# Sample search rounds moved behind a head's masks, summed in the next head; rank sums moved ahead in the last part

## The chip, the cores and the metric

One core of one Trainium2 chip runs the whole program. Its engines are TensorE (PE: matmuls, and weight loads, PEld), VectorE (DVE), ScalarE (ACT), GpSimd (POOL) and SyncE (SP, which issues DMAs). Each runs its own list of instructions in order, and they wait for one another by semaphores. The metric is the device time of one execution in microseconds (us).

## The reference

One step of a hybrid decoder layer on 2048 new tokens of a prompt and on 8 sample tokens that have 4096 cached keys each:

```python
def indexer_scores(q_idx, w_idx, k_idx, valid):
    dots = jnp.einsum("bqhd,bld->bqhl", q_idx, k_idx, preferred_element_type=jnp.float32) * (IDX_DIM ** -0.5)
    s = jnp.einsum("bqh,bqhl->bql", w_idx.astype(jnp.float32) * (N_IDX_HEADS ** -0.5), jax.nn.relu(dots))
    return jnp.where(valid, s, -jnp.inf)
...
    # prompt, by blocks of 128 queries; sample alike, its keys found through a page table
    _, sel = lax.top_k(scores, n_sel)            # n_sel = 256
    att = attend_selected(q, k_sel, v_sel, ...)  # softmax over the selected keys, 8 heads
    conv = z["b_conv"] * short_conv(u_ext, conv_w)
    mo = mem_attend(z["q_mem"], mk, mv)          # 256 memory tokens, 4 heads
    o = concat([att * silu(z["g_att"]), conv * silu(z["g_conv"]), mo * silu(z["g_mem"])]) @ w_out
    return x + rms_norm(o, g_post)
```

The selection of 256 keys is not done by sorting. A threshold is searched bit by bit: count the scores that are not below a candidate, then keep or drop the bit. For the sample, the 4097 scores of each of 8 tokens lie spread over the 128 partitions, so each round of its search has two halves: VectorE counts per partition, and TensorE adds the counts of a token's partitions with a matmul by a matrix of blocks.

## The kernel before

The program has three stretches. The first projects all tokens. The second, on which most of this change works, takes the prompt in 16 parts of 128 queries (j = 0 to 15). The third, called the last part here, finishes the sample. Nothing but the order of each engine's own list and the semaphores sets when things run: the order is written by hand in `b_vector` and `b_tensor` (second stretch) and in `c_vector` and `c_tensor` (last part), with tables that say how many search steps go where.

**A part's heads.** For each of the 8 attention heads h of a part TensorE computes scores of head h+2 (h+1 from part 8 on) into PSUM (L1637). VectorE adds the mask and takes the row maximum (`mask`, L1392, and L1397, which makes the bias of the exponential). ScalarE does the exponential (L1235). TensorE turns the result by transposes (L1647), ScalarE copies the turned blocks out of PSUM (L1216), and TensorE multiplies them with the values (L1655). The probabilities lie in two buffers, so the mask of head h+1 waits for the transposes of head h-1. In head 3 TensorE also turns the memory attention (L1789), into one of the two PSUM slots that the transposes use. VectorE frees it with `gate_mem` (L1482), the first thing that it does in `behind` of head 4.

**What VectorE has besides.** `behind` holds the masks of the next head and a portion of search steps for a later prompt block (L1429, L1432, L1435 a step; select steps at L265 to L290). `normalise` (L1369) scales the output row of the part before, in head 3; GpSimd then adds the residual (L1199), and SyncE stores the row. `take_keys` (L1514, L1518) reads the sample's key products in parts 0 to 2. `decode_round` is one half round of the sample's search, in parts 3 to 7: take the sum of the last round (L1873), set the bit (L1874, L1875), count again (two of L1853), tell TensorE. There are 32 counts, seven in a part and four in part 7. TensorE's half, `decode_total` (L1679), stands at the end of a head, behind its transposes.

**A part's tail.** After head 7 TensorE does the gate products of the next part (L1624), the next block's index products (L1610), the memory scores (L1706) and the output projection (L1715), which all in all keep it busy. VectorE accumulates index scores and does further search steps.

**The last part.** VectorE compares all scores of the sample with the found threshold (L1978, L1980), TensorE sums the counts over partitions (L2125, L2126), VectorE breaks ties by a scan (L1988 to L1998), TensorE sums again (L2129, L2131), VectorE ranks the chosen keys (L2002 to L2007). Then, once ScalarE has gated the sample's projections (L1912, L1913), it prepares the table of chosen places (L2010 to L2026) and builds 64 one-hot blocks (L2048), by which TensorE compacts the places. The gather of keys and values, the attention and the projection follow in a chain. In TensorE's list the gate products of the sample (L2113, 64 matmuls in float32, 128 instructions) and 32 transposes of the memory keys (L2122) stand ahead of the two rank sums.

Of the kernel before, what the change touches and what calls it, by code (L numbers as in the profile page):

```python
# [16 lines left out]
P = 128  # L17
SEQ, D, HD = 2048, 1024, 64
NT = SEQ // P
KD = D // P  # L20
# [1308 lines left out]
def b_vector(dve, m, s):  # L1329
# [208 lines left out]
    def tail(j):  # L1538
        todo = search_steps(j, 1)
        if j >= 0:  # L1540
            take_keys(key_units(j, NH - 1))
            take_att(j)
        for x in range(8):
            behind(j, portion(todo, 8, x) if j < NT - 2 else todo if x == 5 else [], True)
            accumulate(j, x)
            if j + 1 < NT:
                if x == 1:
                    gates(j + 1, 0)
                if x == 3:
                    gates(j + 1, 1)  # L1550
            if x == 3 and j >= 0:
                gate_att(j)
            if x == 3 and j + 1 < NT:
                memory(j + 1)
# [5 lines left out]
    for j in range(NT):  # L1560
# [3 lines left out]
        for h in range(NH):  # L1564
            if h >= 1:
                take_keys(key_units(j, h - 1))
            decode_round(j, h)
# [9 lines left out]
            if h == 3 and j >= 1:  # L1577
                normalise(j - 1)
        tail(j)
# [5 lines left out]
def b_tensor(pe, m, s):  # L1585
# [164 lines left out]
    for j in range(NT):  # L1750
# [19 lines left out]
        for h in range(NH):  # L1770
            if h + ahead < NH:
                scores_of(j, h + ahead)
            for n in key_units(j, h):
                turn_keys(n)
                if before:
                    before()
                before = lambda n=n: times_keys(n)
# [6 lines left out]
            decode_total(j, h)  # L1784
# [316 lines left out]
def c_tensor(pe, m, s):  # L2101
# [9 lines left out]
    for n in range(8 * KD):  # L2111
        b, k = n // KD, n % KD
        mm = pe.matmul(m.bank[3][:, 8 * b:8 * b + 8], m.w2[:, k, b * P:(b + 1) * P], m.xts[:, k, :],  # L2113
                       start=(k == 0), stop=(k == KD - 1))
    mm.then_inc(s.c_z, 1)
# [8 lines left out]
    pe.wait_ge(s.c_sel, 1)  # L2124
    pe.matmul(m.bank[5][:, 4:6], con("blk"), m.cn[:], start=True, stop=True)  # L2125
    pe.matmul(m.bank[5][:, 6:8], con("low"), m.ce[:], start=True, stop=True).then_inc(s.c_off, 1)  # L2126
    pe.wait_ge(s.c_rank_ready, 1)
    for g in range(2):
        pe.matmul(m.bank[5][0:64, 10:11], con("seln")[:, 64 * g:64 * g + 64], m.nsel[:, g:g + 1], start=(g == 0),  # L2129
                  stop=(g == 1))  # L2130
    pe.matmul(m.bank[5][:, 8:10], con("low"), m.cn[:], start=True, stop=True).then_inc(s.c_off2, 1)  # L2131
# [410 lines left out]
```

## Time and profile before

| | us |
|---|---|
| median of three timed runs | 2460.67 (2460.06 to 2463.07) |
| the profiled execution: its own time | 2456.39 |
| its span, from the first to the last instruction | 2454.6 |
| TensorE busy, of the span | 2164.9 |
| VectorE busy | 1414.3 |
| ScalarE busy | 1202.7 |
| granted TensorE clock, mean over the span | 0.878 |

Busy time is a sum over stretches with different limits. The granted clock is 1.0 at 2.4 GHz and 0.5 at 1.2 GHz; a mean between them is a mixture in time. A row of the timeline gives the start in us from the start of the span, the length, the engine and line, and in brackets how long the engine was idle before it and what ended that. A matmul in float32 shows as two instructions.

### The profile page before, as it was taken

What the parts mean: (1) busy time and instruction counts of PE and PEld (TensorE: products, weight loads), DVE (VectorE), ACT (ScalarE), POOL (GpSimd) and SP (SyncE); (2) the same over time, 40 slices, a digit from 0 to 9 for tenths busy, and PEclk for the clock granted to TensorE, in tenths of its full rate; (3) what the DMA queues carried; (4) which work ended last, traced back from release to release, by engine and by line L of the source; (5) the groups of instructions that cost most, each with busy time, mean ns of one, the idle gap of its engine ahead of it and who ended that gap; (6) DMA issues with size and microseconds to landing.
All of it is one profiled execution on the core that took longest, in us unless ns stands there. A gap on an engine that the chain in (4) does not pass through costs nothing. (4 is left out here: it accounts for less than half of the span.)

```text
span 2454.6 us, 33475 instructions
## 1 busy us (share of the span) xinstructions
PE 2164.9 (88%) x12592; PEld 1747.5 (71%) x12592; DVE 1414.3 (58%) x3186; ACT 1202.7 (49%) x2337; POOL 120.5 (5%) x182
## 2 busy tenths in 40 slices
PE   7999999989996889989899898799999889899765
PEld 4776776767765867768678677587687777878662
DVE  2334776667734575675776866557865654343180
ACT  1112467778721345635564565656666566644100
POOL 0000000000000110000000000000000000000004
PEclk9999999999996899986887899789989888898656
DMA  7113121121115423021111110111100100000201
GB/s 276 72 51 102 65 78 54 68 85 45 63 28 199 129 63 107 14 61 48 33 50 39 46 31 32 43 49 46 34 33 20 59 20 29 26 20 23 78 5 31
DMA packets 63344, 144.61 MB, mean 59 GB/s; under 512 B 14456, under 2 KB 28960, under 8 KB 63184
## 3 DMA queue, kind: packets, MB, share of 16 engines
q1 hardware_dynamic: 59856, 131.99, 16.1%
q0 software_dynamic: 3328, 10.49, 1.4%
q8 instruction: 100, 1.64, 0.3%
q14 instruction: 60, 0.49, 0.1%
HBM read 100.22 MB, written 42.24 MB: 58 GB/s over the span
## 5 line engine op out<-in xcount | busy, mean ns | idle before, releaser
L1655 PE MATMUL psum<-sb_v,sb_ptb 128*128 128x64 f32 x2176 | 349.8, 313 | 32.9 <-ACT sb_ptb L1216 32.4
L1655 PEld LDWEIGHTS psum<-sb_v,sb_ptb 128*128 128x128 f32 x2176 | 338.8, 235 | 44.9 <-ACT sb_ptb L1216 44.5
L1216 ACT ACTIVATE sb_ptb<-psum 128x512 f32<-128x512 f32 (+3 forms) x384 | 202.7, 542 | 308.1 <-PE psum L1647 304.2
L819 PE MATMUL psum<-sb_w,sb_xt 128*128 128x512 f32 (+5 forms) x1088 | 337.7, 466 | 0.5 <-DVE sb_xt L552 0.5
L1647 PE MATMUL psum<-sb_con,sb_p 128*128 128x128 f32 x1328 | 247.8, 315 | 52.7 <-ACT sb_p L1235 25.2
L819 PEld LDWEIGHTS psum<-sb_w,sb_xt 128*128 128x128 f32 (+1 forms) x1088 | 183.0, 189 | 127.5 <-issue 114.3
L1647 PEld LDWEIGHTS psum<-sb_con,sb_p 128*128 128x128 f32 x1328 | 184.3, 172 | 84.0 <-ACT sb_p L1235 40.6
L858 PE MATMUL psum<-sb_xt,sb_w 128*128 128x128 f32 x2048 | 237.3, 275 | 0.0
L1392 DVE CUSTOM_DVE_ANT_0 sb_p<-psum,sb_bias 128x1024 f32<-128x1024 f32 (+7 forms) x128 | 126.6, 989 | 190.8 <-PE psum L1637 179.7
L858 PEld LDWEIGHTS psum<-sb_xt,sb_w 128*128 128x128 f32 x2048 | 234.3, 192 | 1.1
L1715 PE MATMUL psum<-sb_wo,sb_mix 128*128 128x512 f32 x512 | 232.4, 597 | 0.0
L297 ACT ACTIVATE sb_lowj<-sb_sc,sb_l_ncand,sb_l_scl 128x1152 bf16<-128x1152 f32 (+7 forms) x128 | 219.7, 1716 | 1.9
L1637 PE MATMUL psum<-sb_ks,sb_qa 128*128 128x512 f32 (+3 forms) x640 | 188.9, 435 | 12.0 <-DVE sb_mx L1392 7.9
L1235 ACT ACTIVATE sb_p<-sb_p,sb_nmax 128x128 f32<-128x128 f32 (+15 forms) x128 | 153.4, 1199 | 68.8 <-DVE sb_nmax L1397 68.5
L1610 PE MATMUL psum<-sb_ks,sb_qi 128*128 128x512 f32 (+3 forms) x448 | 141.4, 434 | 31.1 <-DMA sb_qi<-qt_s 23.1
L1429 DVE TENSOR_SCALAR_CACHE_REDUCE sb_r<-sb_sc,sb_l_c 128x2048 bf16<-128x2048 f32 (+7 forms) x84 | 161.8, 1926 | 0.9
L1715 PEld LDWEIGHTS psum<-sb_wo,sb_mix 128*128 128x128 f32 x512 | 94.9, 191 | 93.7 <-issue 92.5
L1637 PEld LDWEIGHTS psum<-sb_ks,sb_qa 128*128 128x128 f32 x640 | 133.2, 226 | 37.4 <-issue 9.9
L1624 PE MATMUL psum<-sb_p,sb_w 128*128 128x128 f32 x1152 | 145.6, 285 | 0.4
L1624 PEld LDWEIGHTS psum<-sb_p,sb_w 128*128 128x128 f32 x1152 | 143.0, 200 | 4.1 <-issue 0.9
L1610 PEld LDWEIGHTS psum<-sb_ks,sb_qi 128*128 128x128 f32 x448 | 80.7, 195 | 76.1 <-issue 45.9
L1624 PE MATMUL psum<-sb_qa,sb_w 128*128 128x128 f32 x896 | 112.5, 288 | 0.7
(408 smaller groups left out, 2929.3 us busy)
## 6 DMA issues: line engine op xcount, KB each, us to landing
qt_s<-sb_qt SPq DMA_DIRECT2D x32, 512.0 KB, 2.9
sb_x<-in_x_prompt SPq DMA_DIRECT2D x16, 512.0 KB, 4.6
xt_s<-sb_xt SPq DMA_DIRECT2D x16, 512.0 KB, 2.6
sb_qa<-qt_s SPq DMA_DIRECT2D x16, 512.0 KB, 3.6
sb_qa<-qt_s SPq DMA_DIRECT2D x32, 256.0 KB, 4.9
sb_xres<-in_x_prompt SPq DMA_DIRECT2D x16, 512.0 KB, 4.2
out_y_prompt<-sb_y SPq DMA_DIRECT2D x16, 512.0 KB, 2.9
sb_p<-xt_s SPq DMA_DIRECT2D x9, 512.0 KB, 5.6
```

The source lines that it names most:

```text
L297: return act.activation(junk, sc, ACT.Sign, bias=f.ncand[:, p], scale=f.scl[:, p], accum_out=f.tally[:])
L819: mm = pe.matmul(out, m.xt[:, p, k, 0:n], m.w1[:, k, lo:hi], start=(k == 0), stop=(k == KD - 1))
L858: mm = pe.matmul(m.pc[bank][:, j * P:(j + 1) * P], m.w1[:, k, lo:lo + P], m.xt[:, p, k, :], start=(k == 0), stop=(k == KD - 1))
L1216: act.activation(m.ptb[:, g, 0:cols], m.turn[slot][:, 0:cols], ACT.Copy).then_inc(s.t_act, 1)
L1235: act.activation(m.p[:, h % 2, 0:w], m.p[:, h % 2, 0:w], ACT.Exp, bias=m.nmax[:, h:h + 1], scale=SCALE, accum_out=m.l[:, h:h + 1]).then_in ...
L1429: ch.inc(dve.tensor_scalar(junk, sc, f.c[:, p], 0.0, ALU.is_ge, ALU.add, accum_out=f.cnt[:]))
L1610: mm = pe.matmul(m.score2(at)[:, lo:lo + n], m.qi[:, x, h, :], m.ks[:, 0, c[0] + lo:c[0] + lo + n], start=(x == 0), stop=(x == 1))
L1624: mm = pe.matmul(m.turn[slot][:, (b % 4) * P:(b % 4 + 1) * P], m.w2[:, k, b * P:(b + 1) * P], m.xt2(j)[:, k, :], start=(k == 0), stop=(k = ...
L1637: mm = pe.matmul(m.score2(slot)[:, lo:lo + n], m.qa[:, x, h, :], m.ks[:, kv, c[0] + lo:c[0] + lo + n], start=(x == 0), stop=(x == 1))
L1647: mm = pe.transpose(m.turn[slot][:, x * P:(x + 1) * P], src[:, lo + x * P:lo + (x + 1) * P], ident)
L1655: mm = pe.matmul(o, m.ptb[:, g, x * P:(x + 1) * P], v, start=st, stop=sp)
L1715: mm = pe.matmul(m.ybank[:, 512 * x:512 * x + 512], m.mix[:, k, :], m.wo[:, k, 512 * x:512 * x + 512], start=(n == 0), stop=(n == KD - 1))
```

## The change

`decode_round(j, h)` and `take_keys` move from the front of head h to its end, behind the masks of head h+1, the search steps and `normalise`. `take_keys` now names the keys of its own head rather than of the head before; as it stands behind the masks instead of ahead of the next ones, its instructions keep their places. `normalise` moves from head 3 to head 6 in parts 1 to 5. In TensorE's list `decode_total(j, h - 1)` stands in head h behind the scores and ahead of the transposes, where `decode_total(j, h)` stood behind them. In the last part the first rank sum comes ahead of the gate products, the second after 24 of the 64.

```diff
--- before.py
+++ after.py
@@ -1538,7 +1538,6 @@
     def tail(j):
         todo = search_steps(j, 1)
         if j >= 0:
-            take_keys(key_units(j, NH - 1))
             take_att(j)
         for x in range(8):
             behind(j, portion(todo, 8, x) if j < NT - 2 else todo if x == 5 else [], True)
@@ -1562,9 +1561,6 @@
             mask(j, 0, x)
         todo = search_steps(j, 0)
         for h in range(NH):
-            if h >= 1:
-                take_keys(key_units(j, h - 1))
-            decode_round(j, h)
             behind(j, portion(todo, NH, h), False, h + 1 if h + 1 < NH else None)
             if h == 0:
 
@@ -1574,8 +1570,10 @@
                 dve.tensor_tensor(m.mo[:].rearrange("p (h d) -> p h d", h=NMH),
                                   m.mobank.rearrange("p (h d) -> p h d", h=NMH),
                                   m.ml[:].unsqueeze(2).to_broadcast([P, NMH, HD]), ALU.mult).then_inc(s.mo, 1)
-            if h == 3 and j >= 1:
+            if h == (6 if j < 6 else 3) and j >= 1:
                 normalise(j - 1)
+            take_keys(key_units(j, h))
+            decode_round(j, h)
         tail(j)
     decode = c_prepare(dve, m, s, cf)
     normalise(NT - 1)
@@ -1770,6 +1768,7 @@
         for h in range(NH):
             if h + ahead < NH:
                 scores_of(j, h + ahead)
+            decode_total(j, h - 1)
             for n in key_units(j, h):
                 turn_keys(n)
                 if before:
@@ -1781,7 +1780,6 @@
                 if before:
                     before()
                 before = lambda h=h, c=c: times_values(j, h, c)
-            decode_total(j, h)
             if h == 3:
                 pe.wait_ge(s.mo, j + 1)
                 slot = slot_of(turns, ("to", j))
@@ -2108,11 +2106,24 @@
     for h in range(NH):
         pe.transpose(small[:, 64 + 8 * h:64 + 8 * h + 8], m.qpad[:, h, :], id8)
     pe.transpose(small[:, 128:136], m.dsx2[:, 1024:1152], id8).then_inc(s.c_small, 1)
-    for n in range(8 * KD):
-        b, k = n // KD, n % KD
-        mm = pe.matmul(m.bank[3][:, 8 * b:8 * b + 8], m.w2[:, k, b * P:(b + 1) * P], m.xts[:, k, :],
-                       start=(k == 0), stop=(k == KD - 1))
-    mm.then_inc(s.c_z, 1)
+    pe.wait_ge(s.c_sel, 1)
+    pe.matmul(m.bank[5][:, 4:6], con("blk"), m.cn[:], start=True, stop=True)
+    pe.matmul(m.bank[5][:, 6:8], con("low"), m.ce[:], start=True, stop=True).then_inc(s.c_off, 1)
+
+    def gate_products(first, last):
+        for n in range(first, last):
+            b, k = n // KD, n % KD
+            mm = pe.matmul(m.bank[3][:, 8 * b:8 * b + 8], m.w2[:, k, b * P:(b + 1) * P], m.xts[:, k, :],
+                           start=(k == 0), stop=(k == KD - 1))
+        return mm
+
+    gate_products(0, 3 * KD)
+    pe.wait_ge(s.c_rank_ready, 1)
+    for g in range(2):
+        pe.matmul(m.bank[5][0:64, 10:11], con("seln")[:, 64 * g:64 * g + 64], m.nsel[:, g:g + 1], start=(g == 0),
+                  stop=(g == 1))
+    pe.matmul(m.bank[5][:, 8:10], con("low"), m.cn[:], start=True, stop=True).then_inc(s.c_off2, 1)
+    gate_products(3 * KD, 8 * KD).then_inc(s.c_z, 1)
     pe.wait_ge(s.c_mk, 16 * DB)
     for n in range(8):
         if n >= 2:
@@ -2121,14 +2132,6 @@
             t, hp = x // 2, x % 2
             mm = pe.transpose(m.bank[1 + n % 2][:, x * P:(x + 1) * P], m.mk[:, n, t, hp * P:(hp + 1) * P], ident)
         mm.then_inc(s.mk_tr, 1)
-    pe.wait_ge(s.c_sel, 1)
-    pe.matmul(m.bank[5][:, 4:6], con("blk"), m.cn[:], start=True, stop=True)
-    pe.matmul(m.bank[5][:, 6:8], con("low"), m.ce[:], start=True, stop=True).then_inc(s.c_off, 1)
-    pe.wait_ge(s.c_rank_ready, 1)
-    for g in range(2):
-        pe.matmul(m.bank[5][0:64, 10:11], con("seln")[:, 64 * g:64 * g + 64], m.nsel[:, g:g + 1], start=(g == 0),
-                  stop=(g == 1))
-    pe.matmul(m.bank[5][:, 8:10], con("low"), m.cn[:], start=True, stop=True).then_inc(s.c_off2, 1)
 
     pl = m.bank[5][:, 64:112]
     pe.wait_ge(s.c_ranked, 1)
```

TensorE's list in heads 2 and 3 of part 5 before: sums (L1679), scores (L1637), transposes (L1647), values (L1655).

```order
L1679 MATMUL psum<-sb_few,sb_cond 128x2
L1637 MATMUL psum<-sb_ks,sb_qa 128x512 x2
L1637 MATMUL psum<-sb_ks,sb_qa 128x256 x2
L1647 MATMUL psum<-sb_con,sb_p 128x128 x4
L1655 MATMUL psum<-sb_v,sb_ptb 128x64 x2
L1647 MATMUL psum<-sb_con,sb_p 128x128 x2
L1655 MATMUL psum<-sb_v,sb_ptb 128x64 x4
L1679 MATMUL psum<-sb_few,sb_cond 128x2
```

The same place now (the same lines have numbers lower by 2, scores L1635, sum L1677, transposes L1645):

```order
L1635 MATMUL psum<-sb_ks,sb_qa 128x512 x2
L1635 MATMUL psum<-sb_ks,sb_qa 128x256 x2
L1677 MATMUL psum<-sb_few,sb_cond 128x2
L1645 MATMUL psum<-sb_con,sb_p 128x128 x4
L1653 MATMUL psum<-sb_v,sb_ptb 128x64 x2
L1645 MATMUL psum<-sb_con,sb_p 128x128 x2
L1653 MATMUL psum<-sb_v,sb_ptb 128x64 x4
```

The sum stood ahead of the next head's scores; now it stands behind them and ahead of that head's transposes, and is the sum of the round before.

VectorE's list at the end of head 3 of part 5 before: the last small step of the search (L1435 and before), `normalise` (L1369), a round (L1873 to L1853), `gate_mem` (L1482).

```order
L1432 TENSOR_SCALAR sb_l_g<-sb_l_cnt,sb_l_k,sb_con 128x1
L1435 SCALAR_TENSOR_TENSOR sb_l_c<-sb_l_c,sb_con,sb_l_g 128x1
L1369 SCALAR_TENSOR_TENSOR sb_y<-sb_y,sb_gpost 128x1024
L1873 TENSOR_TENSOR sb_few<-psum,sb_few 128x2
L1874 TENSOR_SCALAR sb_few<-sb_few,sb_con 128x2
L1875 SCALAR_TENSOR_TENSOR sb_few<-sb_few,sb_con 128x2
L1853 TENSOR_SCALAR sb_r,sb_few<-sb_scd,sb_few 128x129 x2
L1482 TENSOR_TENSOR sb_mix<-psum,sb_gate 128x256
```

The same place now (round L1871 to L1851):

```order
L1432 TENSOR_SCALAR sb_l_g<-sb_l_cnt,sb_l_k,sb_con 128x1
L1435 SCALAR_TENSOR_TENSOR sb_l_c<-sb_l_c,sb_con,sb_l_g 128x1
L1871 TENSOR_TENSOR sb_few<-psum,sb_few 128x2
L1872 TENSOR_SCALAR sb_few<-sb_few,sb_con 128x2
L1873 SCALAR_TENSOR_TENSOR sb_few<-sb_few,sb_con 128x2
L1851 TENSOR_SCALAR sb_r,sb_few<-sb_scd,sb_few 128x129 x2
L1482 TENSOR_TENSOR sb_mix<-psum,sb_gate 128x256
```

`normalise` is gone from between, the round is one round earlier, and `gate_mem` follows it. `normalise` stands in head 6 of that part now, behind the last masks (L1397) and the step and ahead of round 6:

```order
L1432 TENSOR_SCALAR sb_l_g<-sb_l_cnt,sb_l_k,sb_con 128x1
L1435 SCALAR_TENSOR_TENSOR sb_l_c<-sb_l_c,sb_con,sb_l_g 128x1
L1369 SCALAR_TENSOR_TENSOR sb_y<-sb_y,sb_gpost 128x1024
L1871 TENSOR_TENSOR sb_few<-psum,sb_few 128x2
L1872 TENSOR_SCALAR sb_few<-sb_few,sb_con 128x2
L1873 SCALAR_TENSOR_TENSOR sb_few<-sb_few,sb_con 128x2
L1851 TENSOR_SCALAR sb_r,sb_few<-sb_scd,sb_few 128x129 x2
L248 TENSOR_SCALAR sb_l_g<-sb_l_c 128x1
```

In parts 6 and 7 it stays in head 3, and there too the round follows it.

TensorE's list at the start of the last part before: transposes for the sample (L2109, L2110), gate products, memory keys, rank sums.

```order
L2110 MATMUL psum<-sb_con,sb_c_dsx 128x8
L2113 MATMUL psum<-sb_xts,sb_w 128x8 x64
L2122 MATMUL psum<-sb_con,sb_mk 128x128 x32
L2125 MATMUL psum<-sb_few,sb_cond 128x2
L2126 MATMUL psum<-sb_c_ce,sb_conc 128x2
L2129 MATMUL psum<-sb_c_nsel,sb_conc 64x1 x2
L2131 MATMUL psum<-sb_few,sb_conc 128x2
```

The same place now (L2110, L2111 and L2123, L2125 are the rank sums, L2116 the gate products, L2133 the memory keys):

```order
L2108 MATMUL psum<-sb_con,sb_c_dsx 128x8
L2110 MATMUL psum<-sb_few,sb_cond 128x2
L2111 MATMUL psum<-sb_c_ce,sb_conc 128x2
L2116 MATMUL psum<-sb_xts,sb_w 128x8 x24
L2123 MATMUL psum<-sb_c_nsel,sb_conc 64x1 x2
L2125 MATMUL psum<-sb_few,sb_conc 128x2
L2116 MATMUL psum<-sb_xts,sb_w 128x8 x40
L2133 MATMUL psum<-sb_con,sb_mk 128x128 x32
```

Both rank sums moved ahead of most gate products and of all transposes of memory keys.

## Rows read from the trace of the kernel before

**Rows 1.** The page, parts 1 and 2: busy shares; granted clock by slice.
```profile
PE 2164.9 (88%) x12592; PEld 1747.5 (71%) x12592; DVE 1414.3 (58%) x3186; ACT 1202.7 (49%) x2337; POOL 120.5 (5%) x182
...
PEclk9999999999996899986887899789989888898656
```

**Rows 2.** Waits of the kernel: engine, line waited for, total, times, longest.
```profile
DVE sb_few L1873 <- PE psum L1679: 25.4, 13, 5.1
```

**Rows 3.** Timeline, TensorE, last part: start, length, line, shapes, idle before.
```profile
2290.55 27.48 PE L2113 MATMUL psum<-sb_xts,sb_w 128*128 128x8 f32 x128
...
2324.38 0.36 PE L2126 MATMUL psum<-sb_c_ce,sb_conc 128*128 128x2 f32 x2
...
2327.62 0.59 PE L2129 MATMUL psum<-sb_c_nsel,sb_conc 128*64 128x1 f32 x4 [2.88 <-DVEq L1974]
...
2328.14 0.59 PE L2131 MATMUL psum<-sb_few,sb_conc 128*128 128x2 f32 x2
```

**Rows 4.** Timeline, VectorE, last part.
```profile
2290.55 0.08 DVE L1980 DVE_READ_ACCUMULATOR sb_c_gt<-sb_scd,sb_few 128x1 f32 x1
...
2324.78 0.16 DVE L1988 TENSOR_SCALAR sb_few<-psum 128x2 f32<-128x2 f32 x1 [33.71 <-PE psum L2126]
...
2330.36 0.23 DVE L2012 SCALAR_TENSOR_TENSOR sb_c_gates<-sb_c_gates,psum 128x32 f32<-128x32 f32 x2
...
2339.65 5.50 DVE L2048 TENSOR_TENSOR sb_oh<-sb_c_iota,sb_c_rankb 128x512 bf16<-128x512 bf16 x9
```

**Rows 5.** Timeline, ScalarE, last part.
```profile
2318.21 0.18 ACT L1913 ACTIVATE sb_c_gates<-psum 128x16 f32<-128x16 f32 x1
```

**Rows 6.** Timeline, TensorE, heads of parts 1 and 3 to 7.
```profile
907.03 0.66 PE L1647 MATMUL psum<-sb_con,sb_p 128*128 128x128 f32 x4 [2.53 <-DVE sb_mix L1482]
...
1045.72 0.39 PE L1679 MATMUL psum<-sb_few,sb_cond 128*128 128x2 f32 x2 [2.74 <-DVEq L1856]
...
1133.39 0.33 PE L1647 MATMUL psum<-sb_con,sb_p 128*128 128x128 f32 x1 [1.97 <-DVE sb_mix L1482]
...
1208.18 0.66 PE L1647 MATMUL psum<-sb_con,sb_p 128*128 128x128 f32 x4 [1.39 <-ACT sb_p L1235]
...
1221.81 0.44 PE L1647 MATMUL psum<-sb_con,sb_p 128*128 128x128 f32 x2 [1.51 <-DVE sb_mix L1482]
...
1224.29 1.65 PE L1637 MATMUL psum<-sb_ks,sb_qa 128*128 128x512 f32 x4 [1.02 <-DVE sb_mx L1392]
...
1235.84 1.11 PE L1647 MATMUL psum<-sb_con,sb_p 128*128 128x128 f32 x4 [1.36 <-ACT sb_p L1235]
...
1317.30 1.12 PE L1647 MATMUL psum<-sb_con,sb_p 128*128 128x128 f32 x4 [1.16 <-ACT sb_p L1235]
...
1398.83 1.11 PE L1647 MATMUL psum<-sb_con,sb_p 128*128 128x128 f32 x4 [4.09 <-DVE sb_mix L1482]
```

**Rows 7.** Timeline, VectorE, part 5, heads 3 to 7.
```profile
1216.46 1.28 DVE L1369 SCALAR_TENSOR_TENSOR sb_y<-sb_y,sb_gpost 128x1024 f32<-128x1024 f32 x1
...
1217.85 2.36 DVE L1874 TENSOR_SCALAR sb_few<-sb_few,sb_con 128x2 int32<-128x2 f32 x1
...
1221.33 0.42 DVE L1482 TENSOR_TENSOR sb_mix<-psum,sb_gate 128x256 f32<-128x256 f32 x1 [0.21 <-DVE sb_r L1853]
...
1224.90 0.23 DVE L1874 TENSOR_SCALAR sb_few<-sb_few,sb_con 128x2 int32<-128x2 f32 x1
...
1234.57 0.15 DVE L1397 TENSOR_SCALAR sb_nmax<-sb_mx 128x1 f32<-128x1 f32 x1
```

**Rows 8.** Timeline, GpSimd, part 5, head 4.
```profile
1217.82 2.35 POOL L1199 TENSOR_TENSOR sb_y<-sb_y,sb_xres 128x1024 f32<-128x1024 f32 x1 [12.99 <-DVE sb_y L1369]
```

**Rows 9.** Two stretches of part 5, and parts 3 to 7: busy (instructions), clock.
```profile
1192.00:1209.00 17.00, 14.46 (x96) 11.78 (x96) 12.33 (x39) 9.28 (x21) 0.93 (x3) 1.00 0.12 39
...
1210.00:1220.00 10.00, 10.00 (x46) 9.61 (x46) 8.17 (x20) 3.27 (x7) 2.18 (x1) 0.50 0.01 2
...
1033.00:1418.00 385.00, 343.43 (x1821) 286.13 (x1821) 269.21 (x659) 197.94 (x387) 16.48 (x20) 0.80 0.15 48
```

## The prediction

> **What bounds the kernel now.** I read the busy shares first, then the clock line, the waits and, where the change works, the timelines of two engines side by side. TensorE is busy for 2164.9 of 2454.6 us, VectorE for 1414.3 [rows 1]: TensorE is the bound over the whole, so what counts is where TensorE itself waits, and at which clock it works. The clock line falls under 9 in most slices of the second stretch [rows 1]; in parts 3 to 7, where the sample's search runs, it averages 0.80 [rows 9]. Of two levels 0.5 and 1.0 that makes 2 x 0.20 x 385 = 154 us at 1.2 GHz. The waits show that VectorE stands still for 25.4 us in 13 waits for a round's sum [rows 2]. That is no loss by itself: in these parts TensorE is busy for 343 of 385 us and VectorE for 269 [rows 9]. The one long stretch where nothing but VectorE's wait counts is the start of the last part: VectorE is ready at 2290.63 and waits 33.71 us, until TensorE has done gate products, memory keys and the first rank sum [rows 3, 4].
>
> **The last part.** VectorE's comparison ends at 2290.63 [rows 4] (2290.55 + 0.08), just when the gate products begin, 27.48 us long [rows 3]. ScalarE's gating ends at 2318.39, 0.36 behind their end at 2318.03 [rows 3, 5]. VectorE first uses the gated values at 2330.36 [rows 4], so they lie ready for 12 us; what is late today is the rank sums, which end at 2324.74 and 2328.73 [rows 3]. In the new order the first sum starts at about 2290.7 and takes some 0.7 (two lines at 0.36). VectorE then needs from 2324.78 to about 2327.6, where the second sum starts: 2.8 us [rows 3, 4]. The 24 products ahead of the second sum take 27.48 x 24/64 = 10.3 us, so its counts lie ready when TensorE comes to it. That sum takes 1.1 us (2327.62 to 2328.73) [rows 3]. The gate products end at 2290.7 + 0.7 + 27.48 + 1.1 = 2320.0 and their gating at 2320.4. VectorE's ranks, 1.6 us behind the second sum, are done by 2304 or so. Thus the gated values are last now, and VectorE goes on at 2320.4 instead of 2330.36: 9.95 us earlier. What is moved behind is the memory keys' transposes, which fill the 6.35 us between gate products and first sum [rows 3]. They run beside the place table and the start of the one-hot blocks, VectorE's work from 2330.36 to 2339.65, 9.3 us [rows 4]; TensorE has nothing else there that the blocks need before them. Cover 9.3 against 6.35: cost nothing; were the cover gone, they would give back 6.35. I take off 0.25 for sums at a lower clock: **-9.7** (bounds -10.0 and -9.4 with the cover).
>
> **Parts 1 and 2: no rounds yet, only `normalise` moves.** TensorE waits 2.53 us for `gate_mem` in part 1 [rows 6], for which `normalise`, 1.28 us [rows 7], stands ahead on VectorE. In head 6 TensorE has nothing so near behind it. -1.2 a part: **-2.4** (bounds: 0, if the masks behind it are as near as `gate_mem` was, and -2.6).
>
> **Parts 3 to 7: the rounds.** The work stays the same: 32 counts, 32 sums. Three things move.
>
> First, VectorE's wait for a sum goes, since the sum it takes was made a head earlier. The price is a wait on the other side: TensorE's transposes of head h stand behind the sum of round h-1, whose counts VectorE ends behind the bias of the exponential (L1397), a small step of the search and a round. A round without stall is 1.34 us: from its L1874 at 1217.85 to the end before `gate_mem`, 1221.12, is 3.27, of which the stall is 2.36 - 0.23 = 2.13, and L1873 adds 0.2 [rows 7]. With 0.5 for the step and 0.36 for the sum (that of the last part [rows 3]), the transposes may start 2.2 us behind L1397, against 1.27 today by way of the exponential (1234.57 to 1235.84 [rows 6, 7]): 0.9 later wherever TensorE is already there. Where TensorE is late, as with a head at 1.2 GHz, it is 0. The buffers of probabilities give VectorE a head of slack, so the 0.9 isn't paid anew by each head, but shows at the end of a part's heads.
>
> Second, the stall of 2.13 us in L1874. It lasts as long as GpSimd's residual, which `normalise` releases (2.36 from 1217.85, 2.35 from 1217.82) [rows 7, 8]; the two end together. The stall goes wherever `normalise` goes. I see no row in which a round runs right behind `normalise` without it.
>
> Third, with `normalise` in head 6 round 6 lies behind 1.28 + 2.13 us more, so that TensorE's transposes of head 7 may start 2.2 + 3.4 = 5.6 us behind L1397 at the most, some 3.6 of it later than the exponential and the ordinary step already make it (0.9 counted above, less the lead that VectorE has from waiting no more). Part by part, with that price between 0 and 3.6:
> - Part 3: TensorE's wait for counts of 2.74 [rows 6] goes. VectorE has little idle time here and so little lead: +3.3 in head 7. Sum +0.6.
> - Part 4: the wait for `gate_mem` of 1.97 goes [rows 6]; +1.0 in head 7. Sum -1.0.
> - Part 5: the waits of 1.51 and 1.02 go [rows 6], as `gate_mem` comes 3.4 earlier and so does the mask behind it. In head 7 the wait of 1.36 for the exponential [rows 6] becomes one for count 6, between 0.3 shorter and 2.7 longer as VectorE's lead goes; I take +1.4. Sum -1.1.
> - Parts 6 and 7: `normalise` stays in head 3, and the round behind it is awaited before the transposes of head 4. In part 7 the wait of 4.09 for `gate_mem` [rows 6] ends with the counts, which are done 0.6 us before `gate_mem` is (0.21 + 0.42 [rows 7]); work that stood before the wait now stands behind it. -1.0 for part 7, and -0.5 of the 1.16 in part 6 [rows 6].
>
> Heads of 3 to 7: **-3.0**. With all three head-7 prices at 0 it is -8.7, with all at 3.6 it is +2.1.
>
> **What the clock may do with it.** At 1.2 GHz a matmul of these heads takes 10.00/46 = 217 ns, at 2.4 GHz 14.46/96 = 151 ns [rows 9]. In part 5 the clock was 1.00 up to 1209, through the wait of 1.39 at 1208.18, and 0.50 from 1210 on [rows 6, 9]; I can't read from the rows which wait would keep it. The Trainium skill ("TensorE: Matmul & The Clock Gate", section "HAM oscillation — how this bites in real kernels") says that long waits between bursts of matmuls throttle the engine anew each time, so that each burst starts cold. It speaks against this change, which gathers several short waits into one longer one in head 7 or 4. The trace agrees in so far as the fall above stands behind a wait; by that rule alone the heads lose and the time is that of the third rival, 2460; by the terms above it is 2445.6.
>
> **Sum.** -9.7 - 2.4 - 3.0 = -15.1. The profiled execution took 2456.39 us, 4.3 under the median of the three timed runs; it would take 2441.3, and the median comes to 2460.67 - 15.1 = **2445.6**. Its own bounds: -10.0 - 2.6 - 8.7 gives 2439.4, and -9.4 + 0 + 2.1 gives 2453.4.
>
> **Rivals.**
> 1. The heads give nothing: each wait removed comes back as a wait for a count, parts 1 and 2 with it. For it: VectorE bounds some of these heads. Against it: the waits for `gate_mem` end behind `normalise` or the stall, which go elsewhere. 2460.67 - 9.7 = 2451.0.
> 2. The clock holds longer. For it: most of the waits in [rows 6] go, and the clock is low for 154 us [rows 9]. Against it: new waits come. If a third of the 154 us rises, 51 x 0.89 (TensorE's share) x (1 - 151/217) = -14: 2431.
> 3. The clock falls oftener: one longer wait in head 7 (parts 3, 5) or 4 (parts 6, 7) carries a low clock into the tail, where TensorE is busy throughout. If four parts lose 12 us each of full clock, 4 x 12 x (217/151 - 1) x 0.7 = +15: 2460, no change.
> 4. Slower: the counts become the bound. If VectorE's head is the longer one in all heads with a round, each of 27 sums holds TensorE 0.9, and the five behind `normalise` 3.6: 24 + 18 = +42, less 9.7 and 2.4, 2491. It decides from where the masks have to wait for the transposes that waited for the counts. Against it: TensorE is the busier engine by 74 us in these parts [rows 9].
> 5. The change doesn't do what it says in one respect: `take_keys` keeps its place, so nothing comes of it. That is in all the sums.
>
> **Chances.** Forecast 0.53, rival 1 0.20, rival 2 0.14, rival 3 0.08, rival 4 0.05. Differences under 0.2% (4.9 us) are taken as no change, about what a measurement of this kernel can tell. Faster: forecast, rivals 1 and 2, 0.87, of which 0.03 is taken off for their upper tails: 0.84. No change: that 0.03 and rival 3 but for 0.01, 0.10. Slower: rival 4 and that 0.01, 0.06. The range takes in rival 1, most of rival 2 and the forecast's bounds, and leaves out rivals 3 and 4: 2430 to 2456.
>
> **What would show it.** In the profile of the changed kernel: in the last part VectorE's wait for the first sum falls from 33.7 to under 2 us and a new wait of some 16 us for ScalarE's gating stands ahead of the first use of the gated values (L2012 now); the memory keys lie beside the place table. VectorE's waits for sums (25.4) are near nothing, and TensorE shows waits for counts before the sums, longest in head 7 of parts 3 to 5 and in head 4 of parts 6 and 7. The L1874 of round 6 takes 2.4 in parts 3 to 5, of round 3 in 6 and 7. Wrong would be: the one-hot blocks start as late as before; waits for counts in most heads; or a clock in parts 3 to 7 that is off 0.80 by more than 0.03.

## The result, and the profile after

The changed kernel took 2417.64 us in the median of four runs (2416.12 to 2425.36), the kernel before 2461.87 (2460.06 to 2464.4): a ratio of 0.9826, interval 0.9803 to 0.9849. The gain, 44 us, is three times the forecast of 15, and outside its range. The profiled execution after took 2425.36 (span 2423.6), that before 2456.39: 31.0 of the 44 us can be followed in the two traces. Medians below are of fast runs; one of e4's six runs, its profiled one, is 1.5% above that kernel's fastest and counts as slow.

In the last part the sum came out. VectorE's rows after (as [rows 4] before):

```profile
2269.44 0.08 DVE L1978 DVE_READ_ACCUMULATOR sb_c_gt<-sb_scd,sb_few 128x1 f32 x1
...
2270.69 0.16 DVE L1986 TENSOR_SCALAR sb_few<-psum 128x2 f32<-128x2 f32 x1 [0.72 <-PE psum L2111]
...
2281.97 0.16 DVE L2000 COPY sb_few<-psum 128x2 f32<-128x2 f32 x1 [8.55 <-PE psum L2125]
...
2299.52 0.09 DVE L2008 MEMSET sb_c_qmb<- 128x32 f32 x1 [16.04 <-ACT sb_c_gates L1911]
...
2308.84 11.52 DVE L2046 TENSOR_TENSOR sb_oh<-sb_c_iota,sb_c_rankb 128x512 bf16<-128x512 bf16 x19
```

From the end of its comparison (2269.52, before 2290.63) to the one-hot blocks (2308.84, before 2339.65) it takes 39.32 us where it took 49.02: 9.70 less. The wait for the first sum is 0.72 instead of 33.71, the last of the three waits is the 16.04 for ScalarE's gating. TensorE's memory keys (before between gate products and first sum, [rows 3]) lie beside the place table and end at 2304.93, ahead of the blocks:

```profile
2298.86 3.36 PE L2133 MATMUL psum<-sb_con,sb_mk 128*128 128x128 f32 x16
...
2302.44 1.15 PE L2133 MATMUL psum<-sb_con,sb_mk 128*128 128x128 f32 x8 [0.23 <-ACT sb_kp L1915]
...
2303.78 1.15 PE L2133 MATMUL psum<-sb_con,sb_mk 128*128 128x128 f32 x8 [0.19 <-ACT sb_kp L1915]
```

In part 2 the wait for `gate_mem` was, before:

```profile
973.73 0.52 PE L1647 MATMUL psum<-sb_con,sb_p 128*128 128x128 f32 x3 [2.30 <-DVE sb_mix L1482]
```

In the heads after, first the waits for the transposes of parts 1 and 2, then waits for counts in parts 3 to 7, the longest of each part and for part 3 one more (as [rows 6]):

```profile
909.43 0.66 PE L1645 MATMUL psum<-sb_con,sb_p 128*128 128x128 f32 x4 [1.33 <-DVE sb_mix L1482]
...
974.95 0.52 PE L1645 MATMUL psum<-sb_con,sb_p 128*128 128x128 f32 x3 [1.10 <-DVE sb_mix L1482]
...
1043.71 0.56 PE L1677 MATMUL psum<-sb_few,sb_cond 128*128 128x2 f32 x2 [3.24 <-DVEq L1854]
...
1057.40 0.56 PE L1677 MATMUL psum<-sb_few,sb_cond 128*128 128x2 f32 x2 [4.85 <-DVEq L1854]
...
1142.26 0.56 PE L1677 MATMUL psum<-sb_few,sb_cond 128*128 128x2 f32 x2 [3.21 <-DVEq L1854]
...
1227.81 0.56 PE L1677 MATMUL psum<-sb_few,sb_cond 128*128 128x2 f32 x2 [5.45 <-DVEq L1854]
...
1290.55 0.56 PE L1677 MATMUL psum<-sb_few,sb_cond 128*128 128x2 f32 x2 [4.68 <-DVEq L1854]
...
1385.64 0.35 PE L1677 MATMUL psum<-sb_few,sb_cond 128*128 128x2 f32 x2 [3.46 <-DVEq L1854]
```

In part 1 the wait for `gate_mem` is 1.33 instead of 2.53 and in part 2 1.10 instead of 2.30: 1.2 each, as forecast. The waits for counts of 3.21 and 5.45 (parts 4 and 5) stand in head 7, behind `normalise`; those of 4.68 and 3.46 (parts 6 and 7) stand in head 4, behind the `normalise` of head 3. Those of 3.24 and 4.85 in part 3 were not foreseen: the counts stand there behind select steps, and the scan of the second alone takes 2.62. Part 3's wait of 2.74 [rows 6], which was to go, has thus come back longer. VectorE in part 3 (the scan) and in part 5, head 6 (`normalise`, the stalled L1872, which was L1874; compare [rows 7]):

```profile
1053.21 2.62 DVE L281 TENSOR_TENSOR_SCAN sb_sc<-sb_r,sb_l_tie,sb_l_one 128x1152 bf16<-128x1152 bf16 x1
...
1222.96 1.28 DVE L1369 SCALAR_TENSOR_TENSOR sb_y<-sb_y,sb_gpost 128x1024 f32<-128x1024 f32 x1
...
1224.35 2.34 DVE L1872 TENSOR_SCALAR sb_few<-sb_few,sb_con 128x2 int32<-128x2 f32 x1
```

The waits of the whole kernel by engine, line and releaser (total, times, longest), after: VectorE's waits for a round's sum fall from 25.4 [rows 2] to 4.8, TensorE's for counts come to 28.8.

```profile
PE psum L1677 <- DVEq L1854: 28.8, 9, 5.4
...
DVE sb_c_qmb L2008 <- ACT sb_c_gates L1911: 16.0, 1, 16.0
...
DVE sb_few L2000 <- PE psum L2125: 8.6, 1, 8.6
...
DVE sb_few L1871 <- PE psum L1677: 4.8, 4, 2.5
...
DVE sb_few L1986 <- PE psum L2111: 0.7, 1, 0.7
```

TensorE's waits for counts before:

```profile
PE psum L1679 <- DVEq L1856: 5.8, 3, 2.7
```

So far little seems gained. What was gained shows in the table of stretches. Parts 3 to 7 before (length, then busy time and instructions of TensorE, weight loads, VectorE, ScalarE and GpSimd, granted clock, DMA share, GB/s):

```profile
1033.00:1471.50 438.50, 393.56 (x2103) 324.21 (x2103) 307.56 (x715) 237.19 (x453) 16.48 (x20) 0.82 0.14 43
```

After, and below it a stretch of part 5 at the place where [rows 9] had a clock of 0.50:

```profile
1032.90:1455.90 423.00, 370.39 (x2103) 303.53 (x2103) 306.74 (x719) 235.33 (x452) 16.35 (x20) 0.88 0.15 45
...
1210.00:1220.00 10.00, 8.18 (x61) 6.93 (x61) 8.76 (x36) 5.01 (x11) 0.00 (x0) 1.00 0.00 0
```

These parts take 15.5 us less. TensorE's idle time in them, length less busy time, is 52.6 instead of 44.9: 7.7 more. Its busy time for the same 2103 matmuls is 370.4 instead of 393.6: 23.2 less, at a clock of 0.88 instead of 0.82. (The 0.80 of [rows 9] ends with the heads of part 7; with its tail the same low time gives 0.82.) Added up from the clock record, which is the trace's list of stretches at either level, the time at 1.2 GHz is 102 us there, and was 154.

| trace, after less before | length | TensorE busy | idle | time at 1.2 GHz |
|---|---|---|---|---|
| up to part 0 | -3.4 | -4.2 | +0.8 | -6 |
| parts 0 to 2 | +3.3 | +7.3 | -4.0 | +17 |
| parts 3 to 7 | -15.5 | -23.2 | +7.7 | -51 |
| parts 8 to 14 | -10.8 | -11.2 | +0.4 | -29 |
| part 15 and the last part | -4.6 | +4.9 | -9.5 | -1 |

The last row hides the last part's gain: from VectorE's comparison to the end the kernel takes 154.1 us instead of 164.0, 9.9 less, but part 15 ahead of it is 5.3 longer, with 12 us more at 1.2 GHz. Parts 1 and 2 likewise lose idle time in a stretch that is longer at a lower clock.

### The profile page after: what moved, and what is told of

Same layout as the page of the kernel before. It is cut to its first block and busy times, and to the rows that moved or that the text cites. A ratio compares the mean times of both kernels' runs of the same rounds, so it can differ in the third digit from the quotient of the medians.

```text
span 2423.6 us, 33477 instructions
## 1 busy us (share of the span) xinstructions
PE 2138.6 (88%) x12592; PEld 1725.7 (71%) x12592; DVE 1413.8 (58%) x3186; ACT 1200.7 (50%) x2337; POOL 120.2 (5%) x182
## 5 line engine op out<-in xcount | busy, mean ns | idle before, releaser
L1653 PE MATMUL psum<-sb_v,sb_ptb 128*128 128x64 f32 x2176 | 339.4, 307 | 32.8 <-ACT sb_ptb L1216 32.1
L1653 PEld LDWEIGHTS psum<-sb_v,sb_ptb 128*128 128x128 f32 x2176 | 326.9, 228 | 45.6 <-ACT sb_ptb L1216 44.8
L1645 PE MATMUL psum<-sb_con,sb_p 128*128 128x128 f32 x1328 | 240.1, 307 | 35.2 <-ACT sb_p L1235 20.5
L1645 PEld LDWEIGHTS psum<-sb_con,sb_p 128*128 128x128 f32 x1328 | 181.4, 170 | 60.0 <-ACT sb_p L1235 31.8
L1635 PE MATMUL psum<-sb_ks,sb_qa 128*128 128x512 f32 (+3 forms) x640 | 180.6, 419 | 10.6 <-DVE sb_mx L1392 6.3
L1635 PEld LDWEIGHTS psum<-sb_ks,sb_qa 128*128 128x128 f32 x640 | 127.2, 217 | 34.6 <-issue 9.6
```

Of the source, the lines that this page charges most:

```text
L1635: mm = pe.matmul(m.score2(slot)[:, lo:lo + n], m.qa[:, x, h, :], m.ks[:, kv, c[0] + lo:c[0] + lo + n], start=(x == 0), stop=(x == 1))
L1645: mm = pe.transpose(m.turn[slot][:, x * P:(x + 1) * P], src[:, lo + x * P:lo + (x + 1) * P], ident)
L1653: mm = pe.matmul(o, m.ptb[:, g, x * P:(x + 1) * P], v, start=st, stop=sp)
```

## What a microsecond at the low clock costs

Every timed run carries its span and its mean granted clock c, so 2 x (1 - c) x span is its time at 1.2 GHz. Over the 53 runs of the kernel before, all of one program, spans go from 2439.0 to 2469.8 and time at 1.2 GHz from 553 to 622 us; the line through them rises by 0.39 us for each us at 1.2 GHz. One slope for all 149 runs of the study, with a level for each kernel, is 0.38, and spans lie 2.6 us off it. So a difference of two kernels can be parted: the rest (waits and work) is the median distance of a kernel's runs from the line, less that of the 53 runs, and the clock's share is what is left. Taken as slope times the difference in median time at 1.2 GHz, the clock's share comes out up to 3 us otherwise, so differences of a few us in these two columns tell nothing. Times and differences are medians, to the runs of before in the same batch; the ratio and its 95% interval are estimated on their own and can differ from the quotient of the medians in the third place.

| run | time | ratio (interval) | difference | by the clock | the rest |
|---|---|---|---|---|---|
| e1 last part only | 2445.9 | 0.996 (0.994 to 0.999) | -8.8 | -2 | -7 |
| e2 `normalise` only | 2430.3 | 0.988 (0.983 to 0.992) | -24.4 | -17 | -7 |
| e3 rounds only | 2436.1 | 0.991 (0.988 to 0.994) | -18.6 | -12 | -7 |
| e4 rounds and `normalise` | 2419.5 | 0.985 (0.980 to 0.990) | -35.2 | -32 | -3 |
| e5 the change again | 2411.0 | 0.980 (0.976 to 0.985) | -46.3 | -35 | -11 |
| e6 `normalise` behind round 6 | 2402.2 | 0.978 (0.974 to 0.982) | -55.1 | -38 | -17 |
| e7 before, filler | 2452.1 | 0.997 (0.994 to 0.999) | -5.2 | -15 | +10 |
| e8 change, filler at part starts | 2412.6 | 0.980 (0.976 to 0.984) | -44.8 | -38 | -7 |
| e9 `normalise` in head 2 | 2422.3 | 0.986 (0.982 to 0.989) | -35.5 | -21 | -14 |
| e10 before, without the stall | 2438.3 | 0.992 (0.989 to 0.995) | -19.6 | -14 | -6 |
| e11 change, filler in head 7 | 2411.5 | 0.980 (0.976 to 0.984) | -46.4 | -34 | -12 |
| e12 e6, gate products earlier | 2407.4 | 0.979 (0.975 to 0.983) | -50.5 | -33 | -17 |

The rest of the change (e5), -11, lies between the first rival's -9.7 and the forecast's -15.1; it is the clock, -35, that the forecast put at nothing.

## The experiments

**e1 to e4: the parts of the change alone.** e1 has only `c_tensor` of the change, e3 only this in `b_vector` and `b_tensor` (the `take_keys` ahead of the tail goes too), e4 the same with `normalise` as in the change:

```diff
-            if h >= 1:
-                take_keys(key_units(j, h - 1))
-            decode_round(j, h)
...
+            take_keys(key_units(j, h))
+            decode_round(j, h)
...
+            decode_total(j, h - 1)
...
-            decode_total(j, h)
```

and e2 only this:

```diff
-            if h == 3 and j >= 1:
+            if h == (6 if j < 6 else 3) and j >= 1:
                 normalise(j - 1)
```

> Only the last part's new order, the rest as before. Theory A (each part of the change acts in its own place): VectorE goes on in the last part some 9 us earlier, as the two traces show (8.3 from the last part's start to the end), so 9.7 less, 2452, with TensorE's clock up to the last part as before (0.82 in parts 3 to 7). Rival B (part of the 44 us is drift of the clock that any other order gives): 2425 to 2445, with parts in which nothing is changed shorter too.

> Only normalise moved from head 3 to head 6 in parts 1 to 5; rounds, sums and last part as before. Theory A (the rounds' new order is what lifts the clock of parts 3 to 7 from 0.82 to 0.88): no gain from this alone beyond parts 1 to 5's waits for gate_mem, 2455 to 2461, clock of parts 3 to 7 at 0.82 to 0.84. Rival C (the longest waits, those behind normalise and the stalled round, lower the clock, and moving them is the gain): 2440 to 2448, clock 0.86 or more.

> Only the rounds behind the masks and their sums in the next head; normalise stays in head 3 of all parts, last part as before. Theory A: most of the gain ahead of the last part, 34 us, is here: 2427 to 2435, TensorE's idle time in parts 3 to 7 no shorter than the 44.9 us of before, but the clock there 0.86 or more. Rival C: under 10 us of gain, 2452 to 2460, clock 0.82 to 0.84.

> Rounds, sums and normalise as in the change, last part as before. Theory A: as e3 and some 3 us less for parts 1 and 2, and with the last part's 9.7 it adds up to the whole change: 2427. Rival C: this is the sum of e2 (2444) and e3 (2456), 2440. Rival B (drift): it does not add up with e1, by more than 8 us.

e1: -8.8, theory A by its size (by the interval 3 to 15). e2 fell against A and for C: moving one instruction of 1.28 us gives 24 us, more than C had said (median 2430). e3 alone gives 18.6 where A had 27 to 34 and C under 10. The two overlap: together 35.2, not 43. With e1's 8.8 that is 44.0, against 46.3 for the whole change (e5): the parts add up, which rival B had denied. Parts 3 to 7 in their traces, e2:

```profile
1029.30:1455.60 426.30, 379.02 (x2103) 308.75 (x2102) 307.42 (x715) 237.22 (x452) 16.38 (x20) 0.86 0.15 44
```

e3:

```profile
1042.80:1465.50 422.70, 376.66 (x2103) 309.95 (x2102) 306.83 (x719) 235.08 (x452) 16.35 (x20) 0.86 0.14 45
```

e4:

```profile
1027.30:1457.20 429.90, 378.82 (x2103) 311.79 (x2103) 306.91 (x719) 235.31 (x452) 16.40 (x20) 0.86 0.14 44
```

Each of the two moves has a clock of 0.86 there in its trace, where before had 0.82, and neither takes idle time away: 47.3, 46.0 and 51.1 us against 44.9. Rival B can't be thrown out for the whole: parts 8 to 14, in which these kernels do the same in the same order, have from 114 to 184 us at 1.2 GHz in the thirteen traces without filler there, and the times of one kernel (e1 to e12) spread by 15 to 37 us. But e1, which leaves the heads alone, gains only 2 us by the clock, and a lottery would not put the ratios of all twelve runs, with their intervals, under 1.

**e5: the change again**, for a second trace.

> The changed kernel once more, for a second trace and for the same chip as the next three. Theory D (the moves lift TensorE's clock: a wait in the middle of the heads keeps it low for long, the wait gathered in head 7 is followed by the dense tail and costs a short spell): low-clock time in parts 3 to 7 again 95 to 125 us, against 154 and 147 of the two orders with before's rounds and normalise; idle time of TensorE there again 48 to 55. Rival B (the clock is a lottery): low-clock time anywhere from 90 to 155.

```profile
1024.30:1454.50 430.20, 380.14 (x2103) 312.86 (x2103) 306.86 (x719) 235.33 (x452) 16.33 (x20) 0.86 0.14 44
...
1024.30:1260.80 236.50, 204.46 (x1133) 166.48 (x1132) 169.13 (x436) 121.16 (x251) 9.81 (x12) 0.86 0.15 47
```

Parts 3 to 7 have 123 us at 1.2 GHz this time and parts 3 to 5 the same 68 as in the first trace; idle time is 50.1. That is as theory D said, but 123 lies within rival B's 90 to 155 too; this run does not decide between them.

**e6: `normalise` behind the round.**

```diff
-            if h == (6 if j < 6 else 3) and j >= 1:
-                normalise(j - 1)
             take_keys(key_units(j, h))
             decode_round(j, h)
+            if h == (6 if j < 8 else 3) and j >= 1:
+                normalise(j - 1)
```

> As the change, but normalise stands behind the round of head 6 instead of ahead of it, and in parts 6 and 7 too, so that no count waits for it or for the stall. Theory D: the waits for counts in head 7 of parts 3 to 5 (4.9, 3.2 and 5.5 us in the trace of the change) shrink by about 3.4 each and those in head 4 of parts 6 and 7 (4.7, 3.5) by about 2; low-clock time in parts 3 to 7 under 90; 10 to 20 us faster than e5. Rival A2 (VectorE bounds these heads, so the waits only move): within 5 us of e5.

```profile
1029.90:1437.70 407.80, 366.18 (x2103) 299.29 (x2102) 302.43 (x719) 235.64 (x452) 18.75 (x20) 0.90 0.15 46
```

The waits of 3.2 and 5.5 in parts 4 and 5 and of 4.7 and 3.5 in parts 6 and 7 are gone or 2.4 at most (those of part 3, behind the select steps, stay), idle time is 41.6, time at 1.2 GHz 85. In the trace, which is of the fastest of its six runs (2381.5), these parts are 15 and 22 us shorter than in the two of the change; the medians differ by 8.8, under D's 10, and the intervals overlap. It is the best kernel measured, but by how much is not settled.

**e7: the clock lifted with nothing moved.** Ten transposes of the identity at the start of each part 3 to 7, and ten ahead of head 4's transposes:

```diff
+    def keep(n, out):
+        for x in range(n):
+            pe.transpose(out, ident, ident)
...
+        if 3 <= j < 8:
+            keep(10, m.bank[7][:, 384:512])
...
+            if h == 4 and 3 <= j < 8:
+                keep(10, m.turn[slot_of(turns, ("t", j, h, chunks(width(j), 512)[0]))][:, 0:128])
```

> Before, with nothing moved; ten more transposes of the identity (not read by anything) at the start of each of parts 3 to 7 and ten ahead of the transposes of head 4, beside the waits there. Theory D: low-clock time in parts 3 to 7 falls by 20 us or more and the kernel gets 5 to 15 us faster though TensorE does 100 matmuls more (about 15 us at full clock, if none lay in a wait). Rival E (the waits themselves were the loss, not the clock): the same or up to 15 us slower.

```profile
1044.20:1477.30 433.10, 380.26 (x2203) 312.07 (x2203) 307.41 (x715) 236.99 (x453) 16.37 (x20) 0.89 0.14 44
```

The kernel before does 100 matmuls more and is 5.2 us faster, at the low end of D (by the interval 2 to 15). The clock of parts 3 to 7 is 0.89, time at 1.2 GHz 99 us instead of 154, and TensorE is busy for 380 instead of 394 us with 2203 matmuls instead of 2103. Idle time is 52.8, not less. So the low clock is a cost of its own; rival E falls.

**e8: filler at part starts of the change.** The first of e7's two edits, in parts 3 to 14.

> The change, with ten more such transposes at the start of each of parts 3 to 14, beside a wait of 1.9 to 2.7 us that is behind a fall of the clock in parts 4 and 8 of every trace so far. Theory D: 5 to 15 us faster than e5, low-clock time of part 4's heads under 10 instead of 24. Rival E: the same or up to 10 slower than e5.

Part 4's heads in its trace:

```profile
1097.30:1123.00 25.70, 19.99 (x146) 17.67 (x145) 20.69 (x74) 18.03 (x44) 1.18 (x4) 0.96 0.06 20
```

and in the trace of the change:

```profile
1106.30:1138.80 32.50, 29.76 (x150) 26.57 (x148) 20.54 (x73) 18.24 (x45) 0.95 (x4) 0.63 0.05 17
```

The spell of low clock is gone there, 2 us of it instead of 24, and the heads take 25.7 instead of 32.5. In all of part 4 the time at 1.2 GHz is 14 us instead of 34, but in parts 3 to 5 together 58 instead of 68: parts 3 and 5 have more. The kernel as a whole, 2412.6, is no faster than e5's 2411.0: the forecast for the place held, that for the time failed. By the table the fillers cost 4 us and the clock gave back 3, which is no more than the table can tell.

**e9: `normalise` and its wait in another place.**

```diff
-            if h == (6 if j < 6 else 3) and j >= 1:
+            if h == (2 if 3 <= j < 6 else 6 if j < 3 else 3) and j >= 1:
```

> As the change, but normalise in head 2 instead of head 6 in parts 3 to 5, ahead of the round as in the change, so that the same wait for counts stands in head 3 and not in head 7. Theory D (a wait in the middle of the heads keeps the clock low for longer than the same wait ahead of the tail): low-clock time in parts 3 to 5 up by 15 us or more over the two traces of the change (68 both times), 5 to 12 us slower than the change, ratio to before 0.983 to 0.986 against 0.980. Rival F (only the length of a wait counts, not its place): low-clock time within 8 us of 68, ratio 0.978 to 0.982.

Two of its waits for counts, parts 3 and 5:

```profile
1046.59 0.56 PE L1677 MATMUL psum<-sb_few,sb_cond 128*128 128x2 f32 x2 [6.54 <-DVEq L1854]
...
1210.98 0.35 PE L1677 MATMUL psum<-sb_few,sb_cond 128*128 128x2 f32 x2 [2.20 <-DVEq L1854]
```

and parts 3 to 5 as a whole:

```profile
1032.50:1272.60 240.10, 215.19 (x1133) 178.03 (x1132) 167.87 (x436) 121.10 (x251) 9.82 (x12) 0.80 0.15 46
```

Against e5's second row (236.5 us, idle 32.0) it is idle for 24.9 us, 7 less, and yet takes 3.6 us more, since TensorE is busy 10.7 us longer at 0.80 instead of 0.86: 96 us at 1.2 GHz instead of 68. Ratio 0.9857, in D's range; both of F's numbers fail, though the ratio's interval overlaps that of e5. With less waiting the kernel is slower. That the place of the wait is the reason is shown by one part only: in part 5 the clock is low for 27 us behind the 2.20 in head 3, where it was low for 10 behind the 5.45 in head 7 in both traces of the change. In part 3 it is back after 10 us behind the 6.54 in head 3. In part 4 it falls behind the 1.85 us at the part's start, as in the change, and stays low for 44 us; but it does so for 44 in e6 and 48 in e2 too, so those are no sign of the place.

**e10: the stall alone.** This kernel leaves out the residual of five blocks of output rows but for 8 columns.

```diff
-        pool.tensor_tensor(m.y[:], m.y[:], m.xres[:], ALU.add).then_inc(s.y_sum, 1)
+        cols = slice(0, 8) if 2 <= j < 7 else slice(0, D)
+        pool.tensor_tensor(m.y[:, cols], m.y[:, cols], m.xres[:, cols], ALU.add).then_inc(s.y_sum, 1)
```

> Before, with GpSimd's residual add in parts 3 to 7 cut from 1024 columns to 8 (the residual of five blocks of output rows is left out but for those), so that L1874 does not stall; normalise stays in head 3. Theory G (it is the stall that made the waits in head 4): L1874 takes 0.23 in every round, low-clock time in parts 3 to 7 falls by 20 us or more from 154, 5 to 15 us faster than before. Rival H (the stall is hidden, normalise's own 1.28 us and its place make the gain of the second run): within 4 us of before.

L1874 is L1875 here (durations min, median, max in ns), and below it parts 3 to 7:

```profile
L1875 DVE TENSOR_SCALAR sb_few<-sb_few,sb_con x31: 227/228/254, 1040.3 to 1388.3; 128x2 int32<-128x2 f32 x31
```

```profile
1035.00:1461.60 426.60, 381.43 (x2104) 311.93 (x2103) 296.93 (x715) 237.40 (x453) 5.69 (x20) 0.86 0.14 44
```

No stall (254 ns at most, 2.36 us before), 120 us at 1.2 GHz instead of 154, 19.6 us faster (by the interval 12 to 28): G, with more than it had forecast. Five stalls of 2.13 us, which make 10.7 us of VectorE's time, cost some 20 us of the kernel's.

**e11: filler in the wait ahead of the tail.**

```diff
+            if h == 7 and 3 <= j < 6:
+                keep(20, m.turn[slot_of(turns, ("t", j, h, chunks(width(j), 512)[0]))][:, 0:128])
             decode_total(j, h - 1)
```

> The change, with 20 transposes of the identity (not read by anything) ahead of the sum in head 7 of parts 3 to 5, beside the waits for counts of 4.9, 3.2 and 5.5 us. Theory D: the falls of the clock at the end of the heads of parts 3 and 5 do not come, low-clock time in the tails of parts 3 to 5 under 15 instead of 33 us, at 0.39 us each 5 to 9 us less for the same work, 0 to 3 us back for filler that reaches over the wait: 3 to 8 us faster than the change, which interval of 10 us wide can't tell; the trace decides. Rival E (filler changes nothing but adds work): low-clock time there 28 to 38.

The tails of parts 3 to 5, from the last exponential on, in its trace:

```profile
1052.30:1094.60 42.30, 39.65 (x242) 31.01 (x241) 28.89 (x69) 15.42 (x35) 1.80 (x1) 0.96 0.30 87
...
1130.10:1186.00 55.90, 52.78 (x297) 40.66 (x296) 35.40 (x59) 37.44 (x72) 0.00 (x0) 0.97 0.18 53
...
1213.20:1255.10 41.90, 40.78 (x250) 31.86 (x249) 35.20 (x72) 25.44 (x52) 1.85 (x1) 0.97 0.29 88
```

and in that of the change:

```profile
1060.20:1106.30 46.10, 40.84 (x222) 32.04 (x221) 28.85 (x69) 15.40 (x35) 1.78 (x1) 0.86 0.27 82
...
1138.80:1197.60 58.80, 52.72 (x273) 40.24 (x272) 37.69 (x60) 37.41 (x71) 2.32 (x1) 0.91 0.16 51
...
1223.40:1270.10 46.70, 41.28 (x228) 32.64 (x228) 36.54 (x74) 25.43 (x52) 2.34 (x1) 0.89 0.26 79
```

Time at 1.2 GHz in the three tails is 10 instead of 33 us, and each is shorter, by 2.9 to 4.8 us: 11.5 together, with 60 matmuls more. D's forecast for the tails holds in the trace (the 4.9 of its text was the wait behind the select step in head 6; in head 7 of part 3 it is 2.6). The median does not tell it from e5.

**e12: e6 with gate products ahead of the sample's transposes.**

```diff
+    gate_products(0, 4 * KD)
     pe.wait_ge(s.c_row, 2)
...
-    gate_products(0, 3 * KD)
+    gate_products(4 * KD, 5 * KD)
     pe.wait_ge(s.c_rank_ready, 1)
...
-    gate_products(3 * KD, 8 * KD).then_inc(s.c_z, 1)
+    gate_products(5 * KD, 8 * KD).then_inc(s.c_z, 1)
```

> The sixth run (normalise behind the round of head 6 in parts 1 to 7) with 32 of the 64 gate products ahead of TensorE's wait of 9.5 us for the sample's rows at the start of the last part, 8 between the two rank sums and 24 behind them. If that wait is idle time on the path: TensorE does some 9 us of gate products in it, the gating ends 9 us earlier, and the kernel takes 9 us less than the sixth run, 2393, ratio 0.974 (between 0.970 and 0.978). Rival: the first rank sum comes later behind the products and VectorE's chain is last again: no gain over the sixth run, 0.978.

```profile
2248.08 13.82 PE L2108 MATMUL psum<-sb_xts,sb_w 128*128 128x8 f32 x64 [9.49 <-SPq L2447]
...
2278.45 0.88 PE L2134 MATMUL psum<-sb_con,sb_mk 128*128 128x128 f32 x3
```

In the change the same wait stood ahead of the sample's transposes:

```profile
2268.38 1.01 PE L2107 MATMUL psum<-sb_con,sb_c_qpad 8*128 8x8 f32 x8 [9.48 <-SPq L2446]
```

The wait of 9.49 us now stands ahead of the gate products: it was not for the sample's rows but for SyncE at the border of the two stretches. The memory keys begin 30.4 us behind it, as they did in the change (2298.86 - 2268.38 = 30.5). No gain over e6, for a reason that the rival did not name; I had taken the line behind a wait for its cause.

## Why the prediction was wrong

- *The last part, -9.7*: right, 9.70 in the trace, with the wait that was to be next (16.04 us) and the cover of the memory keys.
- *Parts 1 and 2, -1.2 each*: right in the waits, 2.53 to 1.33 and 2.30 to 1.10; the clock there was lower in this trace and hid them.
- *Heads of parts 3 to 7, -3.0*: the mechanism of the wait in head 7 was right, but its price too small: in part 4 the wait is 3.2 us where the sum had 1.0, in part 5 it is 5.5 where it had 1.36 + 1.4 = 2.8, and 4.1 at most. The 4.68 in part 6 has no price in it. As idle time the heads and tails lost 7.7 us instead of gaining 3. In part 3 select steps stand ahead of counts, which the sum had not looked for: the wait of 2.74 came back as 3.24, and one of 4.85 came new.
- *First rival, each wait removed comes back as a wait for a count*: for TensorE's idle time in parts 3 to 7 this came nearer than the forecast, and more than came back (+7.7).
- *What the clock may do, nothing*: this is the step that failed; the sum had no term for it. The clock was a rival with 14 chances in 100, at 2431, and it is most of the gain: -23.2 us of busy time against +7.7 of idle time in parts 3 to 7. The time there fell by 51 us, as that rival had it for a third of 154; that the size fits is luck, since it was 31 in the second trace of the change. Its price was too low: 0.27 us for each us at 1.2 GHz, from 217 and 151 ns a matmul in two short stretches with different matmuls, where the busy times give 23.2/51 = 0.45 and the runs of before 0.39.
- *Third rival, a longer wait lowers the clock into the tail*: its sign was wrong. The clock does fall behind the gathered wait in head 7 (parts 4 and 5 after), but by the clock record it is back after 10 us both times, in the dense tail (14 and 10 in e5); in the spells among the heads it stays low for 10 to 34 us before, and for 27 in part 6 after. Part 7 varies, 7 after and 27 in e5. The Trainium skill ("TensorE: Matmul & The Clock Gate", section "HAM oscillation — how this bites in real kernels") has long waits between bursts throttle the engine. The fall behind the wait of 5.45 agrees with it; it says nothing of where a wait stands, and in part 5 a wait of 2.20 among the heads cost more low time than one of 5.45 ahead of the tail (e9).
- *Slower, by counts in every head*: did not come; the waits for counts were 28.8 us in nine.

What stays open: why the whole run gains more than parts 3 to 7 show, and which wait starts a long spell and which does not. By the clock of the runs the change has 70 to 94 us less at 1.2 GHz; the traces place 31 to 51 of them there. The others lie in stretches with the same work in the same order, where the clock differs from run to run.

## What to carry to other kernels

Where TensorE is the bound and its clock is not full, price a change by what it does to the clock and not by the waits alone: read low-clock time by stretch, and take its price from runs of one kernel, here 0.39 us for each us. Take more than one trace: the same kernel had 102 and 123 us of it in the same parts. A wait that can't go seems better placed ahead of dense work than among work that has small waits of its own; one part of one trace (e9) shows it here. A stall of one engine is to be followed to the wait of TensorE that it makes longer: 10.7 us of VectorE's cost some 20.

## What the runs showed of the hardware

Matmuls that nobody reads, put into waits, lifted the clock of parts 3 to 7 from 0.82 to 0.89 and made a kernel faster that did more work (e7). An instruction of VectorE on 2 columns took 2.36 us instead of 0.23 beside GpSimd's add, and 0.25 at most when that add had 8 columns (e10). And one program on one core, run on two chips, had spans that spread over 31 us (2439 to 2470 in 53 runs), nearly all of it along the line of the clock.
